# Experts' rows gathered as quarter rows and turned in 32 x 32 squares by VectorE; down projection with k outermost; weights stored in runs of 8 KB

## The reference

```python
logits = xt @ w_router + b_router
top_logit, top_e = lax.top_k(logits, 4)          # 4 of 32 experts for each token
gates = jax.nn.softmax(top_logit, axis=-1)
# for the rows xb of expert e:
gate, up = jnp.split(xb @ w_gate_up[e] + b_gate_up[e], 2, axis=-1)   # 1024 -> 2 x 1024
gate = jnp.minimum(gate, 7.0); up = jnp.clip(up, -7.0, 7.0)
act = (up + 1.0) * gate * jax.nn.sigmoid(1.702 * gate)
y_rows = act @ w_down[e] + b_down[e]                                  # 1024 -> 1024
# y[token] += gate_of_the_choice * y_rows
```

## Time and profile before

| what | before |
|---|---|
| median of 3 runs | 2565.65 us (2564.59 to 2567.39) |
| span of the profiled execution, first to last instruction | 2562.3 us |
| what lies around the span, against the median | 3.35 us |
| PE busy | 2497.7 us, 97% of the span |
| DVE, ACT, POOL busy | 1032.2, 617.9, 212.9 us |
| experts stage, first to last expert matmul | about 806 to 2414 us |
| mean granted TensorE clock | 0.982 of full speed |

### The profile page before, as it was taken

How to read it: one execution, slowest core, us unless ns; L and a number is a source line. 1 busy time by engine, 2 the same in 40 slices (tenths; PEclk the granted TensorE clock), 3 DMA queues, 4 the chain that set the end, 5 groups by cost and what they waited for, 6 DMA issues and landing times. The chain is left out here.

```text
span 2562.3 us, 51308 instructions
## 1 busy us (share of the span) xinstructions
PE 2497.7 (97%) x20593; PEld 2270.5 (89%) x20594; DVE 1032.2 (40%) x1894; ACT 617.9 (24%) x1358; POOL 212.9 (8%) x227
## 2 busy tenths in 40 slices
PE   8999999999998999999999999999999999999898
PEld 6787877797446999999999999999999999999776
DVE  4667618725225222223223332334323323232386
ACT  4434323643111111111111111111111111111265
POOL 0000115352000000000000000000000000000130
PEclk9999997999998999999999999999999999999899
DMA  4111220001715766777888888999999999999562
GB/s 150 40 49 58 91 74 19 18 4 35 262 59 180 260 216 227 239 241 258 274 261 274 277 287 285 298 299 288 303 308 301 307 299 303 309 306 307 192 220 75
DMA packets 438616, 528.58 MB, mean 206 GB/s; under 512 B 11892, under 2 KB 407112, under 8 KB 438472
## 3 DMA queue, kind: packets, MB, share of 16 engines
q1 hardware_dynamic: 425672, 481.08, 57.1%
q0 software_dynamic: 12800, 45.36, 5.9%
HBM read 485.77 MB, written 40.63 MB: 205 GB/s over the span
## 5 line engine op out<-in xcount | busy, mean ns | idle before, releaser
L1852 PE MATMUL ex_psum<-ex_xT,weight_ring_a 128*128 128x134 f32 (+14 forms) x7168 | 895.4, 286 | 0.8 <-ACT ex_xT L1838 0.8
L1852 PEld LDWEIGHTS ex_psum<-ex_xT,weight_ring_a 128*128 128x128 f32 x7168 | 883.2, 191 | 1.0 <-issue 1.0
L1892 PE MATMUL ex_psum<-ex_hT,weight_ring_b 128*128 128x134 f32 (+14 forms) x4096 | 521.7, 286 | 0.0
L1892 PEld LDWEIGHTS ex_psum<-ex_hT,weight_ring_b 128*128 128x128 f32 x4096 | 508.2, 191 | 0.0
L1862 DVE TENSOR_SCALAR ex_gate<-ex_psum,bias_gate_up 128x192 f32<-128x192 f32 x256 | 95.0, 413 | 665.5 <-PE ex_psum L1852 665.3
L1866 DVE TENSOR_SCALAR ex_up<-ex_psum,bias_gate_up 128x192 f32<-128x192 f32 x256 | 95.0, 413 | 401.0 <-PE ex_psum L1852 401.0
L1879 ACT ACTIVATE ex_sig<-ex_gate 128x384 f32<-128x384 f32 x128 | 66.9, 523 | 777.0 <-DVE ex_gate L1862 776.8
L1900 ACT ACTIVATE ex_yT<-ex_psum,bias_down 128x192 f32<-128x192 f32 x256 | 93.6, 416 | 522.0 <-PE ex_psum L1892 522.0
L2188 PE MATMUL project_psum<-n_hi,w_in_hi 128*128 128x512 f32 x464 | 187.0, 403 | 2.9 <-DVE n_lo L507 2.9
L2188 PE MATMUL project_psum<-n_hi,w_in_lo 128*128 128x512 f32 x464 | 181.8, 392 | 0.0
L2188 PE MATMUL project_psum<-n_lo,w_in_hi 128*128 128x512 f32 x464 | 181.6, 391 | 0.0
(11 more groups left out here) (350 smaller groups left out, 2741.3 us busy)
## 6 DMA issues: line engine op xcount, KB each, us to landing
weight_ring_a<-in_w_gate_up SPq DMA_DIRECT2D x224, 1024.0 KB, 5.6
weight_ring_b<-in_w_down SPq DMA_DIRECT2D x128, 1024.0 KB, 5.6
weight_ring_b<-in_w_gate_up SPq DMA_DIRECT2D x32, 1024.0 KB, 5.2
y_dram<-ex_y_a SPq DMA_DIRECT2D x33, 512.0 KB, 4.6
w_in_pieces<-in_w_in SPq DMA_DIRECT2D x29, 512.0 KB, 3.7
y_dram<-ex_y_b SPq DMA_DIRECT2D x20, 256.0 KB, 3.7
project_work<-in_x SPq DMA_DIRECT2D x8, 512.0 KB, 6.8
gates_dram<-project_work POOLq DMA_DIRECT2D x16, 256.0 KB, 2.9
```

Source lines behind the costliest of these rows:

```text
L1852: mm = pe.matmul(self.ps[:, bank, i * CAP:i * CAP + width], w[:, k, i * P:(i + 1) * P], self.xT[:, k, 0:width], start=(k == 0), stop=(k == ...
L1892: mm = pe.matmul(self.ps[:, bank, i * CAP:i * CAP + width], w[:, k, i * P:(i + 1) * P], self.hT[:, k, 0:width], start=(k == 0 and i == 0), ...
```

## The change

- `gather` fetches quarter rows of 1 KB: six indirect transfers (four where narrow), each of 128 quarters. Partition 32a + s of block b receives quarter a of token row 32b + s. To get such a list, `dve_spread` multiplies the summed token numbers into four columns for each block, `pe_fold` brings them to all four groups of partitions with four small bf16 matmuls (two where narrow), and `dve_list` adds the quarter's number.
- `dve_turn_x` and `dve_turn_y` turn x and y on DVE by transposes of 32 x 32 squares, one instruction each; `pe_turn_x`, `act_keep_x`, `pe_turn_y` and `dve_keep_y` are gone. `dve_turn_x` stands at the end of a pass on DVE, `dve_turn_y` after its step c = 2. With this, partition p of tile j of x and y is element 8p + j.
- `pe_down` has k outermost: step c takes two tiles of k and all eight output tiles, in banks 4 to 7. Its weight tile is every eighth column of the slot. `act_down` empties the eight tiles after the last step; `pe_list` waits for that.
- `store` issues four transfers with runs of 1 KB.
- The host stores the weights so that a slot's 8 KB for a partition are one run.
- At the start of `experts`, DVE turns the first x before `dve_order`. `route` turns the down bias with eight small transposes.

```diff
-            src = g.w_down[bass.ds(e, 1)].rearrange("a (k p) n -> p (a k) n", p=P)[:, :, (i - 8) * 256:(i - 7) * 256]
+        pieces, at = (g.w_gate_up, i) if i < 8 else (g.w_down, i - 8)
+        src = pieces[bass.ds(e, 1), at].rearrange("a p n -> (a p) n").rearrange("p (k n) -> p k n", k=slot_tiles(i))
+def weight_pieces(w_gate_up, w_down):
+    gu = w_gate_up[0].reshape(E, P, KT, 2, 4, 256).transpose(0, 4, 3, 1, 2, 5).reshape(E, 8, P, KT * 256)
+    down = w_down[0].reshape(E, 4, 2, P, D).transpose(0, 1, 3, 2, 4).reshape(E, 4, P, 2 * D)
...
+    def gather(self, pool, x, narrow=False):
+        pool.wait_ge(self.listed, x + 1)
+        pool.wait_ge(self.x_turned, x).then_inc(self.rows_free, 1)
+        for b in range(BLOCKS_NARROW if narrow else BLOCKS):
+            pool.indirect_dma_start(out=self.rows[:, b, :], out_offset=None, in_=self.g.xn_dram.rearrange("t (a n) -> (t a) n", a=QUARTERS),
+                                    in_offset=bass.IndirectOffsetOnAxis(ap=self.list[:, b:b + 1], axis=0)).then_inc(self.rows_in, 16)
+    def pe_fold(self, pe, x, narrow=False):
+        pe.wait_ge(self.spread, 2 * x + 2)
+        pe.wait_ge(self.listed, x)
+        for v in range(2):
+            mm = pe.matmul(self.ps[:, self.LIST, 8:8 + BLOCKS_NARROW], self.fold[:], self.spread_a[:, v], start=(v == 0), stop=(v == 1))
+        for v in range(0 if narrow else 2):
+            mm = pe.matmul(self.ps[:, self.LIST, 8 + BLOCKS_NARROW:8 + BLOCKS], self.fold[0:CAP - P, :], self.spread_b[:, v], start=(v == 0), stop=(v == 1))
+    def dve_turn_x(self, dve, x, landed, after, narrow=False):
+        n = BLOCKS_NARROW if narrow else BLOCKS
+        dve.wait_ge(self.rows_in, landed)
+        dve.wait_ge(self.gu_done, after)
+        dve.transpose(self.xT[:, :, 0:n * SQ].rearrange("p j (b s) -> p b j s", s=SQ),
+                      self.rows[:, 0:n, :].rearrange("p b (r j) -> p j b r", r=SQ)).then_inc(self.x_turned, 1)
     def pe_down(self, pe, m, c, width):
-        w = ring_slot(self.g, 8 + c).rearrange("p (k n) -> p k n", k=KT)
+        w = ring_slot(self.g, 8 + c).rearrange("p (k q j) -> p k j q", k=2, j=KT)
+        if c == 0:
+            pe.wait_ge(self.yT_kept, 8 * m + 4)
+        pe.wait_ge(self.h_done, 4 * m + c + 1)
+        for i in range(2):
+            k = 2 * c + i
+            for j, (bank, first) in enumerate(self.DOWN):
+                mm = pe.matmul(self.ps[:, bank, first:first + width], w[:, i, j], self.hT[:, k, 0:width],
+                               start=(k == 0 and j % 2 == 0), stop=(k == KT - 1), skip_group_check=True)
+    def act_down(self, act, m, e):
+        act.wait_ge(self.dn_done, 4 * m + 4)
+        act.wait_ge(self.y_turned, m + 1)
+        for j in (6, 7, 0, 1, 2, 3, 4, 5):
...
+    def dve_turn_y(self, dve, y, narrow=False):
+        dve.wait_ge(self.yT_kept, 8 * y + 4)
+        dve.wait_ge(self.y_out, 16 * QUARTERS * y + 16)
+        dve.transpose(self.y[:, 0:n, :].rearrange("p b (r j) -> p b j r", r=SQ),
+                      self.yT[:, :, 0:n * SQ].rearrange("p j (b s) -> p b j s", s=SQ)).then_inc(self.y_turned, 1)
             def one_pass(e, width, narrow_x):
                 for c in range(4):
+                    x.pe_gate_up(pe, e, e + 1, c, width)
                     if c == 0:
+                        x.pe_list(pe, e + 1, 8 * e + 4, narrow_x)
+                    if c == 1:
+                        x.pe_fold(pe, e + 1, narrow_x)
+                for c in range(4):
                     x.pe_down(pe, e, c, width)
...
         def _(dve):
             x.dve_find(dve, 0, 0)
+            x.dve_spread(dve, 0)
+            x.dve_list(dve, 0, None)
...
+            x.dve_turn_x(dve, 0, x.rows_total(0, False), 0)
             x.dve_order(dve)
```

More of the change, by code:

```diff
@@ L1729, in dve_list @@
         if not narrow:
[L1730 to L1737, removed]
+            n, more = CAP - P, BLOCKS - BLOCKS_NARROW
@@ new lines, in dve_list @@
+    def dve_list(self, dve, x, landed, narrow=False):
+        dve.wait_ge(self.folded, x + 1)
+        if landed is not None:
+            dve.wait_ge(self.rows_in, landed)
+        quarter = self.g.k[:, K_QUARTER:K_QUARTER + 1]
+        with self.nc.allow_low_precision(reason="token numbers, summed in float32"):
+            n = BLOCKS_NARROW if narrow else BLOCKS
+            dve.tensor_scalar(self.list[:, 0:n], self.ps[:, self.LIST, 8:8 + n], quarter, None, ALU.add).then_inc(self.listed, 1)
@@ L1939, in experts, with store @@
+    def store(self, sp, y, region, narrow=False):
+        n = BLOCKS_NARROW if narrow else BLOCKS
+        sp.wait_ge(self.y_turned, y + 1)
+        for a in range(QUARTERS):
+            sp.dma_start(region[0:n * SQ, a * PIECE:(a + 1) * PIECE].rearrange("(b s) r -> s b r", s=SQ),
+                         self.y[a * SQ:(a + 1) * SQ, 0:n, :]).then_inc(self.y_out, 16)
 def experts(nc, g, sem):
@@ L1997, in _ @@
                         if i == 7:
-                            x.store(sp, 8 * e + 4, *rows(e), narrow=first > NARROW)
+                            x.store(sp, e, rows(e), narrow=first > NARROW)
             def load_embedding():
@@ L2015, in _ @@
             for y in range(E - 1, E + 1):
-                x.store(sp, 8 * y + 4, *rows(y), narrow=True)
+                x.store(sp, y, rows(y), narrow=True)
             def body(n, r, e):
@@ L2111, in _ @@
         def _(act):
[L2112 to L2114 removed]
             act.wait_ge(x.order_ready, 1)
[L2116 to L2124 removed]
+            with act.Fori(0, E) as e:
+                expert = x.expert_at(act, e)
+                for c in range(4):
+                    x.act_sigmoid(act, e, c)
+                x.act_down(act, e, expert)
             def body(n, r, e):
[L2127 to L2129 removed]
+                m = n + E
                 for c in range(4):
@@ L2132, in body @@
                 expert = x.expert_at(act, e)
-                for c in range(4):
-                    x.act_down(act, m, expert, c)
+                x.act_down(act, m, expert)
             overflow(act, body)
```

304 lines of the change are left out of this document (117 added, 187 removed).

## The result

The changed kernel takes **2980.78 us** (median of 4 runs, 2979.29 to 2982.17), against 2565.39 us for the kernel before in the same comparison (2564.59 to 2567.39): 1.162 times the time, interval 1.160 to 1.164, 415 us slower. The forecast was 2497 us and the range ended at 2536. The rival of strided loads happened, and it cost more than its price of 2812 us and than the 2907 us beside it.

A forecast was written before the change was run, and what follows sets the result against it. PE's own instruction stream was taken to bound the kernel. Terms -89.8 + 3.8 + 12.9 + 2.5 + 1.5 + 0.7 = -68.4 us gave a 2493.9 us span, plus 3.35 us: 2497 us, range 2482 to 2536.

The forecast's parts named there:

- The rival of strided loads: Down's 4096 weight loads get slower at a stride: 315 us more, 2812 us, or 2907 at twice 111 ns; chance 0.17.
- The open price: loading weights at a stride: Down's weight loads take every eighth column, 32 bytes apart; extra cost taken as 0, since a slower fetch would be hidden.
- up to the first list: In `route`, eight small turns replace two: +0.7 us.
- first to second list, and the clock behind the gap: Start of `experts`: first x turned before the order delays the second list 12.9 us; half clock after PE's gap adds 2.5.
- turns and fold, 32 passes: Expert loop on PE: 816 turns removed, -89.8 us; the fold's small bf16 matmuls added, +3.8 us.
- end: After the last down matmul: eight activations, a DVE transpose and four store issues, +1.5 us (0 to 3).
- Around the span: Whole run: the median of the runs taken as 3.35 us above the profiled span.
- Transposes on DVE: Turning x and y on DVE: 1.8 to 2.9 us for 1536 elements, hidden beside PE's work in the loop.
- Gathers: Six gathers per wide pass instead of two: sixth starts 6.8 us after the first, x ready in time by 44.4 us.
- The second rival: Gathers land late among 8 KB packets, x's transpose about 2 us late in 18 wide passes: 2533 us; chance 0.10.
- the third: Something as long, DMA above all, fills the removed turns' places; passes keep their length: 2587 us; chance 0.02.
- Runs of 8 KB: Weight loads from DRAM in 8 KB runs: PE waits for no load, so faster loads earn nothing except as cover.

## Why the prediction was wrong, point by point

**The step that failed** is "The open price: loading weights at a stride", where I took 0. Its argument was that PE fetches 128 columns of bf16 in 26 ns, a quarter of a float32 record's time, so that a fetch 1.6 times as long would be hidden. Each half is nearly true of bf16: a strided bf16 load takes 59 ns, which is under 111. But the row says nothing of a float32 record, which costs four times a bf16 record at either stride. The 111 ns of a float32 record at unit stride are no cover under which a slower fetch could hide; they grow to 224 to 239 with it. The factor, 2.1 in float32 (224/107) and 2.3 in bf16, was above DVE's 1.6 as well.

**The rival** had the right place and sign and too small a price. It added DVE's 88 ns a load; PE paid 239 - 111 = 128 in narrow passes and 75 (239 - 164) at 192 columns, 116 on the mean (475.4 us between the two spans over 4096). Even the limit of twice 111 was passed. "It decides from 17 ns" was right, and so the chance of 0.17 was the real mistake: the only row with a stride, and the rule of the Trainium skill (Advanced Engine Details and Errata, SBUF Cachelines), both spoke for it, and against it stood a row of another type at unit stride.

**The rest of the sum** can be read from the kernel with unit stride: 2507.51 us, where the sum gave 2497. Its parts, against the span of before:

| part | forecast | measured |
|---|---|---|
| up to the first list | +0.7 | +6.8 (801.20 - 794.37) |
| first to second list, and the clock behind the gap | +15.4 | +10.6 up to the list, 2.0 in pass 0 |
| turns and fold, 32 passes | -86.0 | -73.9 in 31 passes, in which the clock's 2.0 of the row above is counted already, and -1.5 in the last |
| end | +1.5 | +0.6 |
| sum | -68.4 | -57.3 |

- **Around the span** the sum put 3.35 us. In each run whose own time is on record it is 1.7 to 1.9 us (2506.72 and 2505.0 in the kernel with unit stride); the rest was the distance of one execution from the median.
- **Turns.** A wide pass lost 3.1 us (50.16 to 47.05), not 3.4; a narrow one 1.51 to 1.57, not 1.7. With the fold added back, a turn came to some 0.10 us instead of 0.110. That is 7 us over the stage; 2 us more are passes of 134 columns.
- **Transposes on DVE**, priced at 1.8 to 2.9 us: 2.93 to 2.97 us for 1536 elements, 2.01 to 2.03 for 1024, and hidden in the loop, as said. The x of the wide pass shown above:

```profile
1539.61 2.93 DVE L1870 STREAM_TRANSPOSE ex_xT<-ex_rows 128x1536 f32<-128x1536 f32 x1
```

- **Gathers.** The sixth starts 6.3 us behind the first (1530.73 - 1524.44). The x of the row above is turned as soon as gate and up are done, and is needed at 1567.80. The second rival did not occur in the changed kernel: DVE's waits for rows are 11.6 us in the whole run, 6.35 of them at the start and 5.28 in one pass (x at 1974.68), and PE stood still behind neither in the loop. In the kernel of 1 KB runs it occurred once, for 0.52 us. Nor did the third: from the second list to the last PE has no gap, and so no wait for weights.
- **The start.** The mechanism held: the order and the mark behind the transpose, and PE waiting 4.89 us for the mark. On DVE:

```profile
813.19 2.92 DVE L1870 STREAM_TRANSPOSE ex_xT<-ex_rows 128x1536 f32<-128x1536 f32 x1 [6.35 <-DMA ex_rows<-xn_dram,ex_list]
...
832.81 1.76 DVE L1728 TENSOR_TENSOR ex_mark<-constants,place 128x1536 bf16<-128x1536 f32 x1 [2.29 <-issue]
```

  The gap is shorter than the 7.9 us forecast since the step ahead of it ran at a low clock itself (13.55 us where 10.66 was assumed, granted clock 0.77 from 815 to 830 us).
- **Route** cannot be told. In kernels that are the same up to there, the first list started at 795.61, 798.74, 801.20 and 806.45 us.
- **Runs of 8 KB** earned nothing, as said.

What stays open is what stops PE in some passes of 134 columns (the late mark above explains one of them), and what moves the stages ahead by several us from one execution to the next. Why a float32 load takes as long as four bf16 ones was not looked into.

## What to carry to other kernels

Before a layout is given to PE, look at the distance between neighbouring columns of both operands: up to 8 bytes a float32 load is nearly free (6 ns a record), and from 16 bytes on each column costs about 1.8 ns in a float32 load and in moving data of either type. A bf16 load pays a quarter of that, and moving data at 8 bytes was not tried. If the host may permute the weights, let it write the tile as PE reads it; here that turns a loss of 16% into a gain of 2 to 3%. When an operation has no row at its stride and type, don't scale one from another type: the nearest row with a stride, though of another engine, was the better guide.

## What the runs showed of the hardware that was not expected

- A float32 load of 128 columns 16 or 32 bytes apart paces the stream at 224 to 239 ns, whatever the moving width from 108 to 192; at unit stride 107 to 112 ns where the load sets the pace, at 8 bytes 6 ns more.
- A bf16 load costs 26, 33, 59 and 56 ns at 2, 8, 16 and 24 bytes. A strided bf16 load is thus cheaper than a float32 load at unit stride, and costs the same at either level of the clock (60 and 58 ns at 0.50).
- A moving column costs 1.81 ns in float32 at 32 bytes and 1.76 ns in bf16 at 16 bytes: the narrower type does not help there. At unit stride it does, with 56/128 = 0.44 ns in bf16 against (885.85 - 880.62)/(12 x 512) = 0.85 ns in float32.
- PE's granted clock fell from 1.00 to 0.50 while PE was busy throughout: three groups of 64 bf16 matmuls of two columns stood before it (820.86 to 826.20 us), and matmuls of 512 columns before these. With matmuls of 512 columns between groups of 16 it stayed at 1.00, but for a stretch just behind the first float32 group at 32 bytes and one that began late in the second; the 12 filling records behind these groups took 7.09 and 8.28 us instead of 5.40.
- Loops of equal work agree to 0.02 us a pass between executions, but for the passes of 134 columns, while executions of one kernel lie up to 12 us apart (2498.78 to 2510.93 with k innermost): to judge a part of 2 us, lists have to be compared, not times.
